# A three-branch transformer block and a state-space block on one core: the second block's vector work laid out in single steps, and a bias table loaded later

## The reference, cut to what matters

```python
# first block, in both attentions: logits + bias[head, q, s] of the distance q - s
h = rms_norm_2(x, norm_w)
q, k, v, a_gate, u, z, g_a, g_s = split(h @ w_in)
q, k = rms_norm of each head of 64 columns (16 heads of q, 4 of k)
attn = sliding_window_attention(q, k, v, sinks)
y_a = (attn * silu(a_gate)) @ w_attn_proj
y_ssm = s5_ssm(u, ...)              # 64 groups: s[t] = a * s[t-1] + (B u)[t], a complex; y = C s + D u
glu_a, glu_b = split(gelu(y_ssm) @ w_glu + b_glu)
y_s = (glu_a * sigmoid(glu_b) * silu(z)) @ w_ssm_proj
x = x + (sigmoid(g_a) * y_a + sigmoid(g_s) * y_s) @ w_out
```

## Time and profile before

| | |
|---|---|
| median of 3 executions | 3248.9 us |
| lowest and highest of them | 3247.19 and 3253.15 us |
| the profiled execution: its own time | 3252.97 us |
| its span in the profile | 3251.1 us |
| mean granted TensorE clock | 0.985 |
| PE busy | 3100.8 us, 95% of the span |
| PEld (weight loads), DVE, ACT, POOL busy | 82%, 62%, 47%, 2% of the span |
| chain of work that ended last: PE, DVE | 81%, 8% |
| weights moved | 1040 units of 512 KB |

### The profile page before, as it was taken

The page is one execution under the profiler, slowest core; times in us unless marked ns, Lnnn a source line. Parts: engine busy times, 40 slices in busy tenths (PEclk is TensorE's granted clock), DMA queues, the critical chain, the costliest instruction groups (busy, mean ns, idle before and its releaser), DMA issues.

```text
span 3251.1 us, 44827 instructions
## 1 busy us (share of the span) xinstructions
PE 3100.8 (95%) x16254; PEld 2663.2 (82%) x16254; DVE 2021.1 (62%) x2314; ACT 1523.7 (47%) x1972; POOL 60.0 (2%) x100
## 2 busy tenths in 40 slices
PE   8999898999999999989898999999998998999999
PEld 8888777888888888888787888888887887888987
DVE  6576756555555555666655656566656556887664
ACT  5544545544444444545445455555544453333543
POOL 0000000000000000000000000000000100000000
PEclk9999999999999999999999999999999999999999
DMA  8645463655555555544453666666664534554555
GB/s 289 210 149 182 139 204 117 211 193 191 190 188 193 189 191 171 175 153 156 166 171 123 226 215 205 200 218 202 206 199 150 188 107 162 191 197 160 181 188 168
DMA packets 169519, 594.57 MB, mean 183 GB/s; under 512 B 26221, under 2 KB 26409, under 8 KB 166953
## 3 DMA queue, kind: packets, MB, share of 16 engines
q1 hardware_dynamic: 151936, 549.52, 51.4%
q10 hardware_dynamic: 14968, 28.47, 2.5%
q0 software_dynamic: 2480, 14.73, 1.3%
HBM read 579.00 MB, written 15.99 MB: 183 GB/s over the span
## 4 chain that ended last, share of the span: by engine, by line
PE 81%; DVE 8%; issue 3%; ACT 3%; DVEq 2%; DMA 1%; POOL 1%; POOLq 0%; ACTq 0%; SPq 0%
PE acc L646 21%; PE acc L648 21%; PE acc L647 21%; PE acc L654 4%; PE acc L656 4%; PE acc L657 4%; DVE lo L1580 2%; PE tp L665 2%; PE tp L698 1%; ACT hi L1061 1%; DVE sr L2232 1%; PE tp L1004 1%; DMA raw<-in_stream 1%; PE tp L993 1%; ACT lg L1143 1%
## 5 line engine op out<-in xcount | busy, mean ns | idle before, releaser
L1580 DVE TENSOR_TENSOR lo<-raw,hi 128x1024 fp32r<-128x1024 f32 x1040 | 1263.9, 1224 | 916.5 <-ACT hi L1061 907.2
L1061 ACT ACTIVATE hi<-raw 128x1024 fp32r<-128x1024 f32 x1040 | 1094.2, 1058 | 1288.7 <-PE acc L648 1008.8
L646 PE MATMUL acc<-hi,xh 128*128 128x512 f32 (+2 forms) x2528 | 986.8, 390 | 16.6 <-DVE lo L1580 13.3
L648 PE MATMUL acc<-hi,xl 128*128 128x512 f32 (+2 forms) x2528 | 975.2, 386 | 0.0
L647 PE MATMUL acc<-lo,xh 128*128 128x512 f32 (+2 forms) x2528 | 975.2, 386 | 0.0
L646 PEld LDWEIGHTS acc<-hi,xh 128*128 128x128 f32 x2528 | 476.6, 189 | 116.9 <-DVE lo L1580 12.9
L648 PEld LDWEIGHTS acc<-hi,xl 128*128 128x128 f32 x2528 | 476.6, 189 | 95.2
L647 PEld LDWEIGHTS acc<-lo,xh 128*128 128x128 f32 x2528 | 476.9, 189 | 91.9
L654 PE MATMUL acc<-xh,hi 128*128 128x256 f32 x1152 | 337.2, 293 | 16.6 <-DVE lo L1580 12.0
L656 PE MATMUL acc<-xl,hi 128*128 128x256 f32 x1152 | 329.6, 286 | 0.0
L657 PE MATMUL acc<-xh,lo 128*128 128x256 f32 x1152 | 329.2, 286 | 0.0
(11 more groups left out here) (373 smaller groups left out, 2469.2 us busy)
## 6 DMA issues: line engine op xcount, KB each, us to landing
raw<-in_stream SPq DMA_DIRECT2D x1040, 512.0 KB, 4.2
turn_scratch<-made ACTq DMA_DIRECT2D x8, 1024.0 KB, 6.7
gpost<-in_post_g POOLq DMA_DIRECT2D x6, 1024.0 KB, 5.0
rotc<-turn_scratch ACTq DMA_DIRECT2D x8, 512.0 KB, 4.9
rots<-turn_scratch ACTq DMA_DIRECT2D x8, 512.0 KB, 7.1
bpad<-in_b_pad ACTq DMA_DIRECT2D x8, 512.0 KB, 9.2
toep_scratch<-toep_scratch POOLq DMA_DIRECT2D x1, 2286.0 KB, 14.8
y<-in_mem SPq DMA_DIRECT2D x4, 512.0 KB, 7.8
```

Source lines behind the costliest of these rows:

```text
L646: nc.tensor.matmul(o, ah, hi[s][:, k, 0:g.width], start=first, stop=False)
L648: last = nc.tensor.matmul(o, al, hi[s][:, k, 0:g.width], start=False, stop=final)
L1061: nc.scalar.activation(hi[s][:, :, :], raw[s][:, :, :], ACT.Copy).then_inc(hi_done, 1)
L1580: nc.vector.tensor_tensor(lo[s][:, :, :], raw[s][:, :, :], hi[s][:, :, :].bitcast(F32), ALU.subtract).then_inc(split_done, 1)
```

## The change

1. `second_steps()` lays the steps out anew. `w_weights`, `wT` and `wV` stand one unit later. The gate of the attention becomes four steps (`silu`, `ag_mul`, `ag_high`, `ag_low`), and ACT's silu of `ag` and `z` is a step of its own, no longer part of `out`. The chunks start at position 26.5 (before 25) with a pitch of 11.1 units (before 11.3). `back` becomes 6 steps of one operation, `scan` 4 steps of two scans, `forward` 4 steps, `join` 2 steps, each set 0.6 to 0.65 units apart, and `outputs` stands 10.8 units behind `inputs` (before 7.2 * 11.3 / 8.2 = 9.9). Each chunk has six drains of DVE between the first `back` and `states`, before five.
2. The roots of the heads come in two parts: POOL takes q's 32 columns as soon as q's squares are there, and k's 8 columns behind k's squares; DVE waits for each part where it needs it.
3. The spreading and loading of the bias table moves on POOL from ahead of layer 0 to behind layer 0's first mask (L2381 before), and its own mask moves behind those of the scores.

```diff
@@ -183,7 +183,7 @@
     steps = [(1, "head_rows"), (5, "head_turns")]
     for k in range(8):
         at = 6 + 2 * k
-        steps += [(at, "wL", k), (at + 1, "wE", k), (at + 1, "w_weights", k), (at + 2, "wT", k), (at + 3, "wV", k)]
+        steps += [(at, "wL", k), (at + 1, "wE", k), (at + 2, "w_weights", k), (at + 3, "wT", k), (at + 4, "wV", k)]
     names = ["u0", "u1", "ag0", "ag1"] + [f"{a}{n}" for n in range(4) for a in ("ga", "ap")] + ["z0", "z1"]
     names += ["gs0", "gs1", "gs2"]
     at, ends = 0, {}
@@ -193,17 +193,23 @@
     steps = [(ends[name] + (3 if name == "ag0" else 1), "out", name) for name in names[:-1]] + \
         sorted(steps, key=lambda step: (step[0], step[-1] if len(step) == 3 else -1))
 
-    steps += [(ends["ag0"] + 4, "ag_gate", 0), (ends["ag1"] + 2, "ag_gate", 1)]
-    steps += [(0, "turns", 0), (24, "turns", 1)]
-    pitch = 11.3
+    for n, (name, at) in enumerate((("ag0", 4.5), ("ag1", 2.5))):
+        steps += [(ends[name] + at, "silu", name), (ends[name] + at + 1.5, "ag_mul", n),
+                  (ends[name] + at + 2.7, "ag_high", n), (ends[name] + at + 3.9, "ag_low", n)]
+    steps += [(ends[name] + 2.5, "silu", name) for name in ("z0", "z1")]
+    steps += [(0, "turns", 0), (24.5, "turns", 1)]
+    pitch = 11.1
     for c in range(NCT):
-        scan = [(0, "inputs", c), (1, "back", c), (2.8, "scan", c), (4, "forward", c), (5, "join", c),
-                (7.2, "outputs", c), (7.9, "skip", c)]
+        scan = [(0, "inputs", c), (10.8, "outputs", c), (11.4, "skip", c)]
+        scan += [(0.9 + 0.62 * n, "back", c, n) for n in range(6)]
+        scan += [(4.65 + 0.65 * n, "scan", c, n) for n in range(4)]
+        scan += [(7.25 + 0.6 * n, "forward", c, n) for n in range(4)]
+        scan += [(9.7 + 0.6 * n, "join", c, n) for n in range(2)]
         if c + 1 < NCT:
-            scan += [(8.1, "maps", c + 1)]
+            scan += [(12, "maps", c + 1)]
         if c + 2 < NCT:
-            scan += [(7, "turns", c + 2)]
-        steps += [(25 + pitch * c + at * pitch / 8.2, *step) for at, *step in scan]
+            scan += [(11.6, "turns", c + 2)]
+        steps += [(26.5 + pitch * c + at, *step) for at, *step in scan]
     steps += [(ends["gs2"] - 3, "ys", 0), (ends["gs2"] - 2.5, "ys", 1)]
     return woven([SG[name] for name in names], steps) + [("out", names[-1])]
 
...
-                    elif name in ("z0", "z1"):
-                elif step == "ag_gate":
+                elif step == "silu":
+                    n = int(at[0][-1])
+                    if at[0][0] == "a":
+                        act.wait_ge(ag_scaled, n + 1)
+                        nc.scalar.activation(sg2[:, :, :], sg2[:, :, :], ACT.Silu).then_inc(ag_act, 1)
+                    else:
+                        act.wait_ge(z_scaled, n + 1)
+                        nc.scalar.activation(zs[:, 4 * n:4 * n + 4, :], zs[:, 4 * n:4 * n + 4, :], ACT.Silu)\
+                          .then_inc(z_ready, 1)
...
-            nc.vector.tensor_reduce(qss[:, 0:32], sq.rearrange("p (n d) -> p n d", d=64), AX.X, ALU.add)
-            dve.drain()
+            nc.vector.tensor_reduce(qss[:, 0:32], sq.rearrange("p (n d) -> p n d", d=64), AX.X, ALU.add)\
+              .then_inc(q_squares, 1)
...
+                dve.wait_ge(q_roots, 2)
...
                 elif step == "back":
-                    c = at[0]
-
+                    c, n = at
+                    cos_, sin_ = rotc[c % 2][:, :, :], rots[c % 2][:, :, :]
+                    if n == 0:
+                        dve.wait_ge(turns_loaded[c % 2], 32 * (c // 2 + 1))
+                        o = see_turn(dve, pos, STP[f"s{c}_re"])
+                        nc.vector.tensor_tensor(sd[0][:, :, :], o[:, :, :], cos_, ALU.mult)
+                    elif n == 1:
+                        o = tp[STP[f"s{c}_re"] % 2]
+                        nc.vector.tensor_tensor(sr[0][:, :, :], o[:, :, :], sin_, ALU.mult)\
...
+                        nc.vector.tensor_tensor(st[:, :, :], o[:, :, :], sin_, ALU.mult)\
+                          .then_inc(tp_read[STP[f"s{c}_im"] % 2], 1)
+                        dve.drain()
+                    elif n == 4:
+                        nc.vector.tensor_tensor(sd[0][:, :, :], sd[0][:, :, :], st[:, :, :], ALU.add)
+                    else:
+                        nc.vector.tensor_tensor(sd[1][:, :, :], sd[1][:, :, :], sr[0][:, :, :], ALU.subtract)
+                        dve.drain()
                 elif step == "scan":
 
-                    c = at[0]
-                    dve.drain()
-                    for j, s in enumerate(range(4 * c, 4 * c + 4)):
-                        for m in range(2):
-                            nc.vector.tensor_tensor_scan(sr[m][:, j, :], ssm[:, 0, s:s + 1].to_broadcast([P, T]),
-                                                         sd[m][:, j, :], 0.0, ALU.mult, ALU.add)
-                    dve.drain()
+                    c, n = at
+                    m = n // 2
+                    for j in (2 * (n % 2), 2 * (n % 2) + 1):
+                        s = 4 * c + j
+                        nc.vector.tensor_tensor_scan(sr[m][:, j, :], ssm[:, 0, s:s + 1].to_broadcast([P, T]),
+                                                     sd[m][:, j, :], 0.0, ALU.mult, ALU.add)
+                    if n == 3:
+                        dve.drain()
                 elif step == "forward":
+                    c, n = at
+                    cos_, sin_ = rotc[c % 2][:, :, :], rots[c % 2][:, :, :]
+                    if n == 0:
...
+                    else:
+                        nc.vector.tensor_tensor(sr[1][:, :, :], sr[1][:, :, :], cos_, ALU.mult)
+                        dve.drain()
                 elif step == "join":
-                    c = at[0]
-                    dve.drain()
+                    c, n = at
...
+                    else:
+                        nc.vector.tensor_tensor(sd[1][:, :, :], sd[1][:, :, :], sr[1][:, :, :], ALU.add)
+                        dve.drain().then_inc(states, 1)
...
             load_parameters(0, 0)
-            row_ = 12 * TOEP
-            pool.wait_ge(toep_moved, 16)
-            pool.dma_start(toep_scratch[row_:P * row_].rearrange("(p w) -> p w", w=row_),
...
-            pool.wait_ge(bias_loaded, 32)
-
-            nc.gpsimd.affine_select(out=bias[:, :, P:T], in_=bias[:, :, P:T], compare_op=ALU.is_ge, fill=NEG,
-                                    base=0, pattern=[[0, HA + HB], [-1, P]], channel_multiplier=1)\
-              .then_inc(bias_ready, 1)
...
+                if layer == 0:
+                    row_ = 12 * TOEP
+                    pool.wait_ge(toep_moved, 16)
+                    pool.dma_start(toep_scratch[row_:P * row_].rearrange("(p w) -> p w", w=row_),
+                                   toep_scratch[0:row_].unsqueeze(0).to_broadcast([P - 1, row_]))\
+                        .then_inc(toep_spread, 16)
...
+                        .then_inc(bias_loaded, 16)
+                    pool.dma_start(bias[:, 11, :], shifted[:, 11 * TOEP:11 * TOEP + T]).then_inc(bias_loaded, 16)
                 hold(pool, lat_squares, pos.n(1, 1), passed)
...
+                if layer == 0:
+                    pool.wait_ge(bias_loaded, 32)
+                    nc.gpsimd.affine_select(out=bias[:, :, P:T], in_=bias[:, :, P:T], compare_op=ALU.is_ge, fill=NEG,
...
@@ -2432,7 +2460,9 @@
             nc.gpsimd.memset(flat(vpad), 0.0)
             nc.gpsimd.memset(flat(QP), 0.0)
             pool.wait_ge(q_squares, 1)
-            roots(qrs, qss, 1.0 / 64, 40, q_roots)
+            roots(qrs[:, 0:32], qss[:, 0:32], 1.0 / 64, 32, q_roots)
+            pool.wait_ge(q_squares, 2)
+            roots(qrs[:, 32:40], qss[:, 32:40], 1.0 / 64, 8, q_roots)
 
 
 def bucket_rows():
```

More of the change, by code:

```diff
@@ L1465, in _ @@
                     n = int(name[-1])
[L1466 to L1472, removed]
+                    if name in ("ga0", "ga1", "ga2", "ga3"):
                         if n:
@@ L1486, in _ @@
                         gate_out(name, gsv[:, :, n * W:(n + 1) * W])
-                elif step == "ag_gate":
+                elif step == "silu":
[7 more added lines that the diff above has]
+                          .then_inc(z_ready, 1)
+                elif step == "ag_high":
                     n = at[0]
@@ L2198, in _ @@
                           .then_inc(acc_read[g.parity], 1)
-                elif step == "ag_gate":
+                elif step == "ag_mul":
                     n = at[0]
@@ L2206, in _ @@
                     nc.vector.tensor_tensor(part, part, sg2[:, :, :], ALU.mult).then_inc(ag_mul, 1)
+                elif step == "ag_low":
+                    n = at[0]
                     dve.wait_ge(ag_hi, n + 1)
-                    nc.vector.tensor_tensor(gatl[:, 4 * n:4 * n + 4, :], part,
+                    nc.vector.tensor_tensor(gatl[:, 4 * n:4 * n + 4, :], attnT[:, 4 * n:4 * n + 4, :],
                                             gath[:, 4 * n:4 * n + 4, :].bitcast(F32), ALU.subtract)\
@@ new lines, in _ @@
```

(42 more changed lines are left out.)

29 lines of the change are left out of this document (2 added, 27 removed).

## The result

The changed kernel takes 3261.78 us as a median of 7 executions (3259.06 us at the lowest), the kernel before 3250.16 us. The ratio is 1.0035, 95% interval 1.0024 to 1.0046: **slower by 11.6 us**, 7.8 to 15 by the interval. The forecast was slower by 7.5 us at 3256.4, with a range that held the measured time. One execution of the changed kernel in a much slower state of the chip (5335.8 us, clock 0.635) is left out of the comparison.

What follows compares the result with a forecast made beforehand. PE, busy 95% of the span, was taken as the bound. Chunks +24.5, roots -6.9, head pairs -7.0, table -7.6 and +4.5 sum to +7.5 us, so the median goes from 3248.9 to 3256.4 us; range 3237 to 3271.

Steps and rivals of the forecast that it cites:

- The loop of the chunks: In each chunk DVE stands before a split, so PE's outputs wait for states, 37.7 us in all; change +24.5 us.
- The term for the clock: In the chunks, each PE wait over 2 us costs 1.5 us of clock: 12.0 us after, 6.0 before.
- its 3.1 us for a C unit at full clock: PE's 24 matmuls of a C unit were taken to need some 3.1 us at full clock.
- The bpad wait: PE's 4.2 us wait for the bpad transfer falls to 1.4 us, with one more unit ahead of it.
- The other side: Rival: DVE keeps up in the chunks and the waits go; with none, -42.2 us, 3206.7 us; chance 0.20.
- Its bound for the chunks: Lower bound of the chunks' term if DVE keeps up in all of them: -25.2 us.
- The -42.2 for the whole change: Whole change if DVE keeps up in the chunks with no waits: -42.2 us, 3206.7 us.
- Roots of the heads: At the heads, roots in two parts remove PE's 5.4 us wait and 1.5 us of clock: -6.9 us.
- Head pairs: At the head pairs, one unit later removes PE's seven waits for ze: -7.0 us.
- The table: Moving the bias table gains 7.6 us at startup and costs 4.5 us in layer 0.
- the bound of 9.5 us for one load delayed in full: Upper bound of the bias table's cost in layer 0: one load delayed in full, 9.5 us.
- The single steps of the gates: Single steps in the gates were priced at 0; if their cover fails, one operation, about 1.2 us.

Runs made afterwards that it cites:

- the chain early: The changed kernel with back, scan, forward and join of each chunk moved to earlier positions, outputs, start and pitch kept; 0.9898 of the kernel before, 3214 us.
- e8_table_later: The changed kernel with the three bias table transfers moved behind the roots of layer 0's latents; 1.0006 of the kernel before.
- e1_roots_only: The kernel before with only the roots of the heads in two parts; 0.9978 of the kernel before, 7.2 us faster.
- e5_back_together: The changed kernel with all six back operations at 0.9 units behind the inputs, all else kept; 1.0001 of the kernel before.

## Why the prediction was right or wrong

**The loop of the chunks** was right in its mechanism and near in its size: +24.5 forecast, +23.2 in the traces, and 25 us between the changed kernel and the same with the old layout. DVE waits before the split until t0 + 4.3, as forecast, and the eight waits sum to 36.1 us against 37.7. The term for the clock was too small by 2 us: the stretch grew by 23.2 and its waits by 36.1 - 21.0 = 15.1, so the clock took 8.1 more, where the forecast had 12.0 - 6.0 = 6.0. No row shows its 3.1 us for a C unit at full clock; two of them took 5.7 us. The bpad wait was set at 1.4 us and is 0: the inputs stand two units later, not one, and 5.7 us is more than 4.2.

**The other side was mis-stated.** The rival that DVE keeps up was given the form "if the first split finds its `hi` ready". The run with back together did that and gained only 12 us. The forecast counted the work behind the first lock and did not ask for a second. Its bound for the chunks, -25.2 us against before, was sound: with the chain early they took 319.7 us, 22.5 less than the 342.2 of before. The -42.2 for the whole change was not reached, 33 us by the medians and 38.8 by the spans: the chunks fell 2.7 us short of their bound, and the table gave nothing where the forecast had 3.1.

**Roots of the heads**: -6.9 forecast, -8.0 in the traces, -7.2 alone. Right, PE's wait for ACT's copies behind it unchanged. The -8.0 is read across layers whose time varies by some 5 us between profiles (see the sum), so the -7.2 is the firmer number.

**Head pairs**: -7.0 forecast, -8.8 in the traces. Alone it is -5.9, since PE then arrives earlier at `bpad`. That the gain holds in full in the changed kernel is due to the later start of the chunks. The 1.8 us beyond the seven waits are not accounted for; a part may be the transposes behind them, which are also shorter (0.60 us against 0.66 for four).

**The table**: -7.6 and +4.5 forecast, -8.5 and +8.4 in the traces. The first was right, with both startup waits gone, and the table alone showed its cause: the loads of 30 to 47 us land after a median of 6.0 us now, against 13.9. The step that failed is "the nearest rows are startup's two waits, mean 3.0 us". The loads of the ckv group land after a median of 10.5 us from 131 to 145 us, against 4.4, and the bound of 9.5 us for one load delayed in full was the nearer row, since a lap there has under 1 us to spare. PE's wait there was forecast as 2 to 4 us for `lo` and is 5.39 us for `rs_wide`, an operation that stands behind a late split in DVE's order. The chain of ACT and DVE shows it:

```profile
143.30 1.06 ACT L1067 ACTIVATE hi<-raw 128x1024 fp32r<-128x1024 f32 x1 [7.85 <-DMA raw<-in_stream]
144.39 1.23 DVE L1584 TENSOR_TENSOR lo<-raw,hi 128x1024 fp32r<-128x1024 f32 x1 [8.27 <-ACT hi L1067]
145.53 0.29 DVE L1795 COPY rs_wide<-small 128x256 f32<-128x256 f32 x1
```

The Trainium skill's rule (DMA: Bandwidth & Descriptors, Queues, rings and completion order) is that the engines take turns between queues by packets. Read as the prediction read it, it would have given 0 for the move, and the traces give -0.1 for the two ends together; but it says nothing of the place, and the place of e8_table_later is worth 6 us by the traces and 9 by the medians.

**The sum**: +7.5 forecast, +6.3 between the two profiled executions and +11.6 (7.8 to 15) between the medians. The stretch from about 250 us to the transposes of k has the same code in e1_roots_only and e5_back_together, and took 2341.7 and 2346.8 us in their profiles, so two single profiles cannot tell 6 from 11. The forecast was near partly since its errors cancelled: table +3.0, heads and pairs -2.9, chunks -1.3.

**The single steps of the gates** cost nothing that a row of the changed kernel shows. With the old positions one of them made PE wait 2.54 us, more than the 1.2 us that the forecast named as the price.

## What to carry to other kernels

Where an engine works through one list in which its own chain and a paced stream (here the splits) are mixed, each piece of the chain is locked to the pace of the stream at its position, however idle the engine is. Spreading a chain evenly over the time until its result is needed turns all its slack into locks: put each piece right behind the last stream item that is sure to be ready, let the chain finish early, and keep the slack at its end. Ask for the next lock once the first is removed.

A transfer that shares with a stream may cost less by its size than by the room of the stream where it lands: the same table cost 8.4 us in one place of this kernel and 2.7 in another. Compare the lap of the buffers with the load time there before it is moved.

## What of the hardware was not expected

A wait of PE does not cost a fixed amount of clock. Behind two waits of 3.53 us in the same run of the changed kernel the stretches were (columns as in the earlier trace rows):

```profile
2767.00:2777.00 10.00, 8.67 (x40) 7.55 (x41) 5.35 (x6) 0.00 (x0) 0.00 (x0) 1.00 0.92 318
2808.97:2818.50 9.53, 9.53 (x33) 7.96 (x33) 4.07 (x4) 0.00 (x0) 0.00 (x0) 0.71 0.91 311
```

The first stayed at the clock of 2.4 GHz, the other fell to 1.2 GHz for more than half of the stretch, and its 16 records took 6.42 us instead of 3.72. Over the eight waits the clock cost 15.2 us, by PE's busy time against the run with the chain early, or 1.9 us each. Why the first was spared stays open.
